# The first two tiles of the retention stage projected together, chunk by chunk

## The reference, cut to what matters

```python
h = rmsnorm(x, norm_mix_pre)                      # (2048, 1024)
rq, rk, rv, rg, ... = split(h @ w_in)             # 4 heads of 128, so 512 columns each
rq, rk = rope(rq), rope(rk) * 128 ** -0.5
# over the frames, with a decay for each head:
scores = (q @ k.T) * decay
o = scores @ v + (q * decay_to_row) @ state
state = decay_of_block * state + (k * decay_from_row).T @ v
ret_out = silu(rg) * rms_normalize(o)
```

## Time and profile before

| | us |
|---|---|
| three executions | 2830.57, 2836.14, 2837.41 (median 2836.14) |
| the profiled execution | 2835.72 |
| its span, first to last instruction | 2833.9 |
| TensorE matmuls busy | 2765.2 (98%) |
| VectorE busy | 1491.3 (53%) |
| ScalarE busy | 818.3 (29%) |
| GpSimd busy | 282.1 (10%) |

### The profile page before, as it was taken

How to read it: one execution, slowest core, us unless ns; L and a number is a source line. 1 busy time by engine, 2 the same in 40 slices (tenths; PEclk the granted TensorE clock), 3 DMA queues, 4 the chain that set the end, 5 groups by cost and what they waited for, 6 DMA issues and landing times.

```text
span 2833.9 us, 38651 instructions
## 1 busy us (share of the span) xinstructions
PE 2765.2 (98%) x14321; PEld 2278.4 (80%) x14321; DVE 1491.3 (53%) x3035; ACT 818.3 (29%) x1690; POOL 282.1 (10%) x428
## 2 busy tenths in 40 slices
PE   6999999999979999999999999999999999999998
PEld 5888888778757777667788888888888989898987
DVE  5334334443168888877554444444675444545445
ACT  3112113001046666666322112121241212221212
POOL 1121121222121111110000000000031000000001
PEclk9999999999979999999999999999999999999999
DMA  6444445885742211012311111111232111111123
GB/s 212 105 121 107 109 106 166 186 183 154 196 147 78 86 60 61 31 49 96 130 45 56 49 45 44 59 44 44 67 124 94 45 45 44 44 44 51 38 66 116
DMA packets 381615, 251.40 MB, mean 89 GB/s; under 512 B 252896, under 2 KB 332256, under 8 KB 381504
## 3 DMA queue, kind: packets, MB, share of 16 engines
q1 hardware_dynamic: 289056, 214.14, 25.4%
q0 software_dynamic: 6912, 25.17, 2.9%
q10 hardware_dynamic: 85536, 10.63, 2.4%
HBM read 185.19 MB, written 64.68 MB: 88 GB/s over the span
## 4 chain that ended last, share of the span: by engine, by line
PE 67%; DVE 2%; issue 1%; DMA 1%; ACT 1%; POOL 0%; SPq 0%; POOLq 0%; DVEq 0%
PE bank L2336 25%; PE bank L2376 23%; PE bank L1645 6%; PE bank L1615 4%; PE bank L1673 4%; PE bank L1658 2%; PE bank L2389 1%; PE bank L2418 1%; DVE mix_S L1477 0%; PE bank L2327 0%; DVE mix_S L1506 0%; DVE ffn_x L2131 0%; DVE mix_mTl L1532 0%; PE bank L1628 0%; DMA ffn_x<-x_scratch 0%
## 5 line engine op out<-in xcount | busy, mean ns | idle before, releaser
L2336 PE MATMUL bank<-ffn_hTh,ffn_uph 128*128 128x512 f32 (+3 forms) x1280 | 449.1, 351 | 0.3 <-DVE ffn_upl L2118 0.3
L2336 PE MATMUL bank<-ffn_hTh,ffn_upl 128*128 128x512 f32 (+3 forms) x1280 | 446.6, 349 | 0.0
L2336 PE MATMUL bank<-ffn_hTl,ffn_uph 128*128 128x512 f32 (+3 forms) x1280 | 446.6, 349 | 0.0
L2202 DVE TENSOR_TENSOR ffn_facc<-bank,ffn_facc 128x512 f32<-128x512 f32 x464 | 312.6, 689 | 203.5 <-PE bank L2376 192.7
L2376 PE MATMUL bank<-ffn_dnh,ffn_hidh 128*128 128x512 f32 x960 | 374.8, 390 | 1.7 <-DVE ffn_facc L2202 1.7
L2376 PE MATMUL bank<-ffn_dnh,ffn_hidl 128*128 128x512 f32 x960 | 374.4, 390 | 0.0
L2376 PE MATMUL bank<-ffn_dnl,ffn_hidh 128*128 128x512 f32 x960 | 374.2, 390 | 0.0
L209 PE MATMUL bank<-retw_whi,proj_hTh 128*128 128x512 f32 x760 | 300.9, 396 | 8.5 <-DVE retw_wlo L196 8.4
L209 PE MATMUL bank<-retw_whi,proj_hTl 128*128 128x512 f32 x760 | 297.8, 392 | 0.0
L209 PE MATMUL bank<-retw_wlo,proj_hTh 128*128 128x512 f32 x760 | 297.4, 391 | 0.0
L2336 PEld LDWEIGHTS bank<-ffn_hTh,ffn_uph 128*128 128x128 f32 x1280 | 240.5, 188 | 33.8 <-issue 12.6
(11 more groups left out here) (213 smaller groups left out, 4026.6 us busy)
## 6 DMA issues: line engine op xcount, KB each, us to landing
ffn_raw<-in_w_up_dram SPq DMA_DIRECT2D x64, 512.0 KB, 4.3
ffn_raw<-in_w_down_dram SPq DMA_DIRECT2D x64, 512.0 KB, 3.7
retw_raw<-in_w_in_dram SPq DMA_DIRECT2D x28, 512.0 KB, 5.1
ffn_x<-x_scratch SPq DMA_DIRECT2D x21, 512.0 KB, 5.0
retp_x<-in_x_prompt_dram SPq DMA_DIRECT2D x16, 512.0 KB, 5.1
rows_scratch<-proj_hTh SPq DMA_DIRECT2D x16, 512.0 KB, 2.7
rows_scratch<-proj_hTl SPq DMA_DIRECT2D x16, 512.0 KB, 3.9
dp_kst<-in_cache_diff_k_dram SPq DMA_DIRECT2D x128, 64.0 KB, 3.0
```

The source lines that it names most:

```text
L2202: nc.vector.tensor_tensor(out=part, in0=Dn[i % s.rd][:], in1=part, op=ALU.add).then_inc(s_add, 1)
L2336: last = nc.tensor.matmul(bank[:, 0:w], l[:, k, f * P:(f + 1) * P], r[:, k, c:c + w], start=(k == 0 and q == 0), stop=(k == 7 and q == 2))
```

## The change

Tiles 0 and 1 are taken together. Tile 1 gets row buffers of its own (`hi[1]`, `lo[1]`, formerly of the second part alone) and two more PSUM banks for its transposes. TensorE projects chunk 0 for both tiles, then chunk 1 for both, then chunk 2 and 3 for tile 0, its attention, and chunk 2 and 3 for tile 1; tile 1's transposes stand in the middle of the first chunk. The other streams' orders for the two tiles are written out to match. In SyncE's, the stores of the two q blocks stand between the weight loads. From tile 2 on the order is the old one. In the second part, a memset of GpSimd moves behind its first job. `rotate`, `scale_k`, `o_rstd`, `put_k`, `o_meansq`, `terms`, `blocks` and `attend` are old lines made into functions; `back` is the second half of VectorE's old body, from the wait for the scores on.

```diff
 sync:
-        wt.load(sp, wv, 0, slice(0, 4))
-        sp.dma_start(rope[0][:], rv[0][:, 0:192]).then_inc(s_rope[0], 16)
-        pre.load(sp, xv[1], 1)
-        wt.load(sp, wv, 0, slice(4, 8))
-        wt.load(sp, wv, 0, slice(8, 12))
-        sp.dma_start(decay[:], ret_tab[:, 0:4 * P]).then_inc(s_decay, 16)
-        wt.load(sp, wv, 0, slice(12, 16))
+        wt.load(sp, wv, 0, slice(0, 1))
+        pre.load(sp, xv[1], 1)
+        wt.load(sp, wv, 0, slice(1, 4))
+        for u in range(2):
+            sp.dma_start(rope[u][:], rv[u][:, 0:192]).then_inc(s_rope[u], 16)
...
-        ahead(0, 1, 0, True)
-        ahead(1, 1, 1)
+        wt.load(sp, wv, 0, slice(4, 8))
+        put(0, 0, 0, block=1)
+        wt.load(sp, wv, 0, slice(8, 12))
+        put(1, 1, 0, block=2)
+        wt.load(sp, wv, 0, slice(12, 16))
+        sp.dma_start(decay[:], ret_tab[:, 0:4 * P]).then_inc(s_decay, 16)
+        for t in range(2):
+            store_rows(t, t)
+            pre.load(sp, xv[t + 2], t, t + 3)
+        put(0, 0, 1, range(2), block=3)
+        get(0, 1, 0, 0, True)
+        get(0, 1, 0, 1, True)
+        put(1, 1, 1, range(2), block=4)
...
+        get(1, 1, 1, 0)
+        get(1, 1, 1, 1)
+        store(1, 1, 0)
+        store(2, 1, 1)
 gpsimd:
+        rotate(1, 0)
+        rotate(2, 0)
+        rotate(3, 1)
+        pool.wait_ge(s_qk, 3)
+        scale_k()
+        pool.wait_ge(s_kg, 1)
+        rotate(4, 1)
+        pre.pool_rstd(pool, 0, 3)
+        o_rstd(0)
...
 scalar:
+        pre.act_meansq(act, 0, 1, 1)
+        pre.act_hi(act, 0, 1)
+        wt.act_hi(act, slice(0, 1))
+        pre.act_meansq(act, 1, 1, 2)
+        wt.act_hi(act, slice(1, 4))
+        pre.act_hi(act, 1, 2, pair=1)
+        wt.act_hi(act, slice(4, 14))
+        put_k(0, 3)
+        wt.act_hi(act, slice(14, 16))
+        put_k(1, 4)
...
 vector:
+        pre.dve_xn(dve, 0, 1)
+        pre.dve_lo(dve, 0, 1)
+        wt.dve_lo(dve, slice(0, 1))
+        pre.dve_xn(dve, 1, 2)
+        wt.dve_lo(dve, slice(1, 4))
+        pre.dve_lo(dve, 1, 2, pair=1)
+        wt.dve_lo(dve, slice(4, 6))
+        dve.wait_ge(s_rope[0], 16)
+        terms(1, 0, 0, 0)
+        wt.dve_lo(dve, slice(6, 8))
+        blocks(1, 0)
+        wt.dve_lo(dve, slice(8, 9))
+        dve.wait_ge(s_rope[1], 16)
+        dve.wait_ge(s_put[0][0], 64)
+        terms(2, 0, 1, 1)
+        wt.dve_lo(dve, slice(9, 10))
+        blocks(2, 0)
+        wt.dve_lo(dve, slice(10, 12))
+        terms(3, 1, 0, 0)
+        wt.dve_lo(dve, slice(12, 13))
+        blocks(3, 1)
+        wt.dve_lo(dve, slice(13, 14))
+        dve.wait_ge(s_put[1][0], 64)
+        terms(4, 1, 1, 1)
+        wt.dve_lo(dve, slice(14, 15))
+        blocks(4, 1)
+        wt.dve_lo(dve, slice(15, 16))
+        pre.dve_xn(dve, 0, 3)
+        dve.wait_ge(s_small, 16)
+        dve.wait_ge(s_decay, 16)
+        back(0, 1, 0, lo_next=False)
+        back(1, 1, 1)
 tensor:
+        pre.pe_transpose(pe, ident[:], 1)
+        pe.wait_ge(pre.s_lo, 2)
+        project(0, 0, 0, by_piece=True, halfway=lambda: pre.pe_transpose(pe, ident[:], 2, 1, 1))
+        pe.wait_ge(pre.s_lo, 4)
+        project(0, 1, 1)
+        pe.wait_ge(s_ropeq, 1)
+        project(1, 0, 0, by_piece=True)
+        pe.wait_ge(s_ropeq, 2)
+        project(1, 1, 1)
+        pe.wait_ge(s_ropeq, 3)
+        project(2, 0, 0, by_piece=True)
+        pe.wait_ge(s_S, 1)
+        pe.wait_ge(s_ropeq, 4)
+        project(3, 0, 1, by_piece=True)
+        attend(0, 1, 0, state[0])
+        project(2, 1, 0)
+        pe.wait_ge(s_S, 2)
+        pe.wait_ge(s_g, 1)
+        project(3, 1, 1)
+        pre.pe_transpose(pe, ident[:], 3, 0)
+        attend(1, 1, 1, state[0])
```

More of the change, by code:

```diff
@@ L205, in project @@
         for k in range(kt):
+            if halfway and k == kt // 2:
+                halfway()
             if by_piece and k % self.deep == 0:
@@ L392, in body, with put_k @@
                 pre.pool_rstd(pool, u2, t2 + 1)
[L393 to L396, removed]
+            rotate(2 * t + 1, 0)
+            rotate(2 * t + 2, 1)
             pool.wait_ge(s_qk, 2 * t + 2)
[L398 to L407, removed]
+            scale_k(8 if dec_tile else 4)
+            o_rstd(t)
+        rotate(1, 0)
[7 more added lines that the diff above has]
+        o_rstd(0)
+        pool.wait_ge(s_qk, 4)
+        pool.wait_ge(s_st, 1)
+        scale_k()
+        o_rstd(1)
+        tiles(pool, nt // 2, body, 1)
         body(nt, nt // 2 + 1, 0, True)
     def scalar(act, next_weights):
[L411 to L422, removed]
+        def put_k(u, block):
+            act.wait_ge(s_block, block)
             for a in range(2, 4):
@@ L436, in body @@
                 pre.act_hi(act, 0, t2 + 1)
[L437 to L445, removed]
+            o_meansq(t)
         tiles(act, nt // 2, body, 1)
@@ L449, in vector, with terms @@
     def vector(dve, next_weights):
[L450 to L456, removed]
+        def terms(count, i, u, bank):
+            dve.wait_ge(s_z, count)
+            z, zs = rope_views(Z[bank][:], 4, 64)
+            cos = rope[u][:, 0:64].unsqueeze(1).to_broadcast([P, 8, 64])
+            sin = rope[u][:, 64:192].rearrange("p (a d) -> p a d", a=2).unsqueeze(1)\
+                .to_broadcast([P, 4, 2, 64])
+            nc.vector.tensor_tensor(out=rope_a[i][:].rearrange("p (h d) -> p h d", d=64),
+                                    in0=Z[bank][:].rearrange("p (h d) -> p h d", d=64), in1=cos,
+                                    op=ALU.mult)
+            nc.vector.tensor_tensor(out=rope_b[i][:].rearrange("p (h a d) -> p h a d", a=2, d=64),
+                                    in0=zs, in1=sin, op=ALU.mult).then_inc(s_ropeq, 1)
@@ new lines, in blocks, with front @@
+        def blocks(count, i):
+            dve.wait_ge(s_qk, count)
+            nc.vector.transpose(out=rope_b[i][:], in_=(qn, kn)[i][:]).then_inc(s_block, 1)
+        def front(t, n, u, dec_tile=False):
+            if not dec_tile:
+                t2, n2, u2 = following(t, n, u)
+                pre.dve_xn(dve, u2, t2 + 1)
+            dve.wait_ge(s_rope[u], 16 * n)
+            for i in range(2):
+                dve.wait_ge(s_put[i][1 - u], 64 * n - 64 * (1 - u))
+                terms(4 * t + 1 + i, i, u, i)
+                blocks(2 * t + i + 1, i)
+            if dec_tile:
+                next_weights[0](dve)
@@ L457, in body, with back @@
+        def back(t, n, u, dec_tile=False, lo_next=True):
             S = state[1 if dec_tile else 0]
             length = dec if dec_tile else P
[L459 to L486, removed]
             dve.wait_ge(s_sc, t + 1)
```

116 lines of the change are left out of this document (82 added, 34 removed).

## The result

The changed kernel takes 2843.37 us (median of 12 runs, 2840.11 to 2847.26), the kernel before beside it 2834.95 (12 runs, 2830.57 to 2838.58): ratio 1.0029, 95% interval 1.0022 to 1.0036, or 8.4 us more: a small difference, but the interval lies clear of 1. Forecast were 2843.5 and 7.8 more. The profiled execution took 2847.26 us, the most of the twelve, with a span of 2845.0.

The account below looks back on a forecast made before the run. TensorE, busy 98% of the span, was taken to bound the kernel. Waits on rope terms move the end of tile 1's attention from 85.8 to 93.6, 7.8 us later: 2835.72 becomes 2843.5, range 2833 to 2853.

Parts of the forecast that it names:

- The first: Before chunk 1 of tile 1: TensorE idle 6.4 us for q1's rope terms, which stand behind w8's late load.
- The second: w12's load stands behind block 2 and four q1 stores, at 46.7; k0's terms at 47.7 cost nothing.
- The third: Before chunk 3 of tile 0: k1's terms wait for k0's stores until 64.5; TensorE idle 11.3 us.
- The mark: End of tile 1's attention: 85.8 us before the change, forecast at 93.6, 7.8 later.
- Issuing four stores in a quiet queue: SyncE's four stores of a q block ahead of the next weight loads: 2.58 us, or 5.67 behind loads.
- from w12's landing to that of the stores: SyncE's queue ahead of chunk 3 of tile 0: 4.98 MB at 360 GB/s, 13.8 us, from 50.7 to 64.5.
- The half clock at the start: TensorE's first half chunk at half clock: 2.7 us extra.
- (a): Same mechanism, dearer: SyncE's stores cost 1.4 rather than 0.65, or the queue drains slower; +8.5 to +17 us, chance 0.36.
- the sum: Profiled execution of 2835.72 us with tile 1's attention ending 7.8 later: 2843.5; +4.8 to +8.5 had chance 0.36.
- (b): k0's stores overtake the rows and x in the queue: no change, +0.2 us; -3 to +4.8, chance 0.17.
- (c): Chunk 3 of tile 0 starts before 58.0: faster us for us, down to -15.1 (2820.6); chance 0.11.
- Behind 100 us: After the second tile the timelines stay the old ones, shifted; a difference arising there would show the prediction wrong.

Follow-up runs that it names:

- k0's stores first: Changed kernel with SyncE issuing k0's stores and tile 0's qT and kT loads ahead of the row stores and x2, x3; 2836.89 us, 1.0005 of the kernel before.
- all three repairs: Changed kernel with SyncE's weight loads and k0's stores moved ahead, own buffers for tile 1's blocks, tile 2's scaling behind tile 0's second half; 2821.86 us.
- both orders: Changed kernel with SyncE's weight loads ahead of the q stores and k0's stores ahead of rows and x; 2832.29 us, 0.9992 of the kernel before.
- both orders with own buffers: Changed kernel with SyncE's weight loads and k0's stores moved ahead and tile 1's rotated blocks in two idle output buffers; 2829.97 us, 0.9984 of the kernel before.
- The changed kernel with tile 2's scaling behind: Changed kernel with only VectorE's scaling of tile 2's x moved behind tile 0's second half; 2843.65 us, 1.0026 of the kernel before.

## Why the prediction was right, and where it was off

**The waits, one by one.** The first: w8's load was forecast for 33.5 and issued at 33.40, landed 37.3 (37.5), the terms of q1 ended at 40.85 (41.2), TensorE idle 6.2 (6.4). The second: w12 issued at 45.88 (46.7). The third: k0's stores landed at 64.25 (64.5), TensorE went on at 65.65 (65.8) after 10.96 us (11.3), its chunk took 7.8 us (7.8) because of the half clock. The mark moved by 7.2 us (7.8): 6.6 from the schedule, 0.6 because the norm's gain landed later in this execution. Every step up to the second tile held within a microsecond, and the experiments confirm the two orders by taking them away: the order of weight loads and stores is worth 4.2 us at the mark, the rows ahead of k0's stores 6.0. Together they give 8.0. Where chunk 3 of tile 0 starts they still add up (3.5 and 7.6 us earlier alone, 11.9 together, from the first product); behind it the wait for the decayed scores and its half clock take back more than full clock in chunk 3 gives.

**Where luck helped.** Counted from the first product the steps came 0.7 to 1.2 us earlier than forecast (w8's load 18.4 against 19.1, k0's stores 49.2 against 50.1, the mark 78.0 against 79.2); the late gain hid 0.6 us of that. And the forecast difference of 7.8 us meets the measured 8.4 closely, while the schedule that I can show gives 6.6. The mechanism was right, but agreement this close is partly luck.

**Terms that were mis-sized.** Issuing four stores in a quiet queue took 1.95 us the second time, not 2.58, and from w12's landing to that of the stores it was 64.25 - 50.00 = 14.3 us for 4.98 MB, or 350 GB/s; I had taken 360. The two nearly cancel. The half clock at the start was put at 2.7 us; in the changed kernel full clock was back at 19.03, 4.0 us behind the first product, so it cost 2.0.

**The rivals.** (a), dearer stores, did not come: the two groups took 2.60 and 1.95 us, with nothing under way ahead of them. (Its lower end, +8.5 us, is 2844.2 by the 2835.72 of the sum; the 2844.6 given counts from the median.) (b), stores that overtake the rows, is refuted by the trace (10.1 and 10.8 us to landing) and by the moved stores (2.2 and 2.6). (c), the faster side: chunk 3 of tile 0 had to start before 58.0. With k0's stores first it started at 57.38 and the time was level, as that point says; with all three repairs the way was free and the gain 16.4 us from the first product, against the 15.1 given as its limit. The limit had 2.7 us for the half clock at the start, and in that execution it cost only 1.5, with full clock 3.0 us behind the first product (5.25 in the kernel before).

**What I missed.** That VectorE's scaling of tile 2 stands ahead of tile 0's decayed scores, and needs x2. I had listed it behind the wait for k0's stores and not asked what it waits for itself. In the changed kernel it costs nothing; in k0's stores first, both orders, and both orders with own buffers it took 2.3, 3.4 and 6.7 us of TensorE, and my expectations for the last two missed by it.

**Behind 100 us.** I had named a difference there as a sign against the prediction, and the profile has one: of 11.1 us more span 7.2 are at the mark and 3.8 arise between the first product of the mixing (794.44 and 801.73) and a group of MLP products, which begins at 1397.00 and 1408.13. There the clock was at half for longer. The 36 us from the start of the mixing, before and after:

```profile
794.00:830.00 36.00, 23.29 (x84) 14.71 (x86) 29.19 (x128) 20.72 (x69) 8.37 (x25) 0.57 0.64 210
```

```profile
801.00:837.00 36.00, 22.65 (x76) 14.20 (x77) 28.79 (x127) 20.73 (x69) 8.35 (x25) 0.50 0.62 202
```

And 72 MLP products just ahead of that group, alike in both, took 16.34 us before (from 1375.22) and 17.91 after (from 1384.79), in both behind a wait for a load.

That stretch, from the first product of the mixing to that group, was 602.56 us before, 606.40 after, and 602.96, 601.75, 602.36, 604.03, 603.47, 602.75, 602.78, 603.40 and 602.86 in the profiles of the nine experiments, eight of which contain the change. So 606.40 is the odd one of eleven single executions and no property of the change that I can show. The medians differ by 8.4 us where the schedule explains 6.6; the interval (6.2 to 10.2 us) holds that, and whether the 1.8 are more than noise stays open. The changed kernel with tile 2's scaling behind, the same schedule in all that counts, gives 8.0 between the medians and 7.2 at the mark.

## What to carry to other kernels

When work is moved ahead, follow each queue's written order, DMA queues above all: a load written behind a store waits for the store's data, and a small store written behind megabytes lands behind them. Give the queue what the bound engine needs next, and the bulk that nobody needs soon last. Then ask of each instruction that now has slack what it waits for itself and who stands behind it: three repairs gave 8, 13 and 23 us from the changed kernel only as each next wait was taken away too.

## What the runs showed of the hardware

ScalarE's two stores of k0 went out on its own DMA queue and took 10.8 us to land with the rows and x ahead on SyncE's, where SyncE's own two, issued in the same microsecond and a half, took 10.1; without the rows ahead it was 2.6 and 2.2. So a second issuing engine did not get its stores past the first one's bytes. The queues' packets from 58 to 59 us show why (packets, MB, share of the 16 DMA engines; q10 is ScalarE's, since all that it moved from 45 to 66 us were the 0.13 MB of these two stores):

```profile
q1 hardware_dynamic: 112, 0.39, 96.3%
q10 hardware_dynamic: 112, 0.01, 9.1%
```

The two queues were served packet for packet, and one of ScalarE's carries some 128 bytes, one of SyncE's some 3.5 KB. With SyncE's small packets beside them ScalarE's went seven times as fast (763 from 54 to 55 us with k0's stores first). Why none of them shows before 57 us, 4 us behind their issue, stays open. The Trainium skill has, in "DMA: Bandwidth & Descriptors", section "Issuing engines are not separate DMA queues", that DMAs of all engines run on the same 16 DMA engines and interleave; this trace agrees. I had expected ScalarE's two to land early.

The time at half clock differed between executions where the instructions are the same: in the first 36 us of the mixing (granted clock 0.57 and 0.50) and behind TensorE's first product, where full clock came 4.0 us behind it in the changed kernel and 3.0 in the last of the repairs. So a single profile can't settle differences of 1 us at the start, or of 4 us far from the edit.
